# Where the hi parts of the gate weights are made, stream values in the gate's bank, and four buffers for FoX values

## The reference

```python
h = _rms(x, p['norm_mix'])
(fq, fk, fv, fg, bq, bk, bv, iq, ik, iw, cqa, ckva, ckpe) = jnp.split(h @ p['w_in'], ...)
...                                    # A: FoX, 6 heads, decay by a cumulated log gate
...                                    # B: DSA, 4 heads, indexer scores, top-k keys
...                                    # C: MLA, 6 heads, latent of 128, rotary key
ya = _over_query_blocks(fox_block, fq, qpos_b, cum[:, P:])
yb = _over_query_blocks(dsa_block, bq, qpos_b, iq, iw)
yc = _over_query_blocks(mla_block, q_nope, q_pe, qpos_b)
g = jax.nn.sigmoid((h @ p['w_gate']).astype(f32)).astype(x.dtype)
ga, gb, gc = jnp.split(g, 3, axis=-1)
x = x + (ga * ya @ w_fox_out + gb * yb @ w_dsa_out + gc * yc @ w_mla_out) @ p['w_o']
x = x + (jax.nn.silu(gt) * up) @ p['w_ffn_out']
```

## Time and profile before

| | |
|---|---|
| median of three runs | 2154.47 us |
| the profiled execution | 2154.84 us, its span 2153.0 us |
| PE busy | 2099.4 us, 98% |
| DVE busy | 1392.0 us, 65% |
| ACT busy | 968.7 us, 45% |
| PE on the chain that ended last | 89% of the span |
| chain: DVE 4%, ACT 3%, issue 2%, DMA 1% | |
| DMA | mean 97 GB/s |

### The profile page before, as it was taken

The page is one execution under the profiler, slowest core; times in us unless marked ns, Lnnn a source line. Parts: engine busy times, 40 slices in busy tenths (PEclk is TensorE's granted clock), DMA queues, the critical chain, the costliest instruction groups (busy, mean ns, idle before and its releaser), DMA issues.

```text
span 2153.0 us, 36860 instructions
## 1 busy us (share of the span) xinstructions
PE 2099.4 (98%) x13616; PEld 1883.8 (87%) x13616; DVE 1392.0 (65%) x2833; ACT 968.7 (45%) x2056; POOL 395.1 (18%) x287
## 2 busy tenths in 40 slices
PE   9999999999999999999999999999999999999999
PEld 8998768878979989989899887787889899899897
DVE  4567875545839838838445678766367497396493
ACT  4236766556425424314232467665663353243241
POOL 1120020200004314314011200203000142242230
PEclk9999999999999999999999999999999999999999
DMA  6233224132332222222232332241423222222222
GB/s 217 78 106 127 83 83 124 59 112 104 119 106 79 79 79 80 88 79 89 77 137 76 110 114 88 79 133 55 149 76 135 72 92 86 79 79 88 72 96 79
DMA packets 90681, 207.83 MB, mean 97 GB/s; under 512 B 20676, under 2 KB 46920, under 8 KB 90184
## 3 DMA queue, kind: packets, MB, share of 16 engines
q1 hardware_dynamic: 90504, 205.48, 28.3%
HBM read 181.50 MB, written 23.95 MB: 95 GB/s over the span
## 4 chain that ended last, share of the span: by engine, by line
PE 89%; DVE 4%; ACT 3%; issue 2%; DVEq 1%; POOL 1%; DMA 1%; SPq 0%; ACTq 0%
PE ps L879 28%; PE ps L925 16%; PE ps L1404 8%; PE ps L1406 8%; PE ps L1405 8%; PE ps L937 6%; PE ps L1096 2%; PE ps L1116 2%; PE ps L995 1%; PE ps L1014 1%; PE ps L1040 1%; PE ps L1210 1%; PE ps L1384 1%; PE ps L1175 1%; POOL rsq L1939 1%
## 5 line engine op out<-in xcount | busy, mean ns | idle before, releaser
L1465 ACT ACTIVATE w_hi<-raw 128x1024 fp32r<-128x1024 f32 (+4 forms) x172 | 171.0, 997 | 398.4 <-PE ps L879 369.4
L1994 DVE TENSOR_TENSOR w_lo<-raw,w_hi 128x1024 fp32r<-128x1024 f32 (+4 forms) x124 | 139.1, 1123 | 187.7 <-ACT w_hi L1465 183.8
L925 PE MATMUL ps<-h_hi,w_hi 128*128 128x320 f32 x768 | 246.8, 321 | 1.5 <-ACT g L1465 1.5
L925 PE MATMUL ps<-h_hi,w_lo 128*128 128x320 f32 x768 | 237.7, 310 | 0.0
L925 PE MATMUL ps<-h_lo,w_hi 128*128 128x320 f32 x768 | 237.6, 309 | 0.0
L1404 PE MATMUL ps<-th_hi,op_hi 128*128 128x320 f32 x640 | 198.1, 310 | 3.8 <-issue 3.8
L1939 POOL TENSOR_TENSOR rsq<-ssq,mhalf 128x12 f32<-128x12 f32 (+3 forms) x56 | 118.0, 2107 | 447.7 <-DVE ssq L2072 385.1
L1406 PE MATMUL ps<-th_hi,op_lo 128*128 128x320 f32 x640 | 198.2, 310 | 0.0
L1405 PE MATMUL ps<-th_lo,op_hi 128*128 128x320 f32 x640 | 198.0, 309 | 0.0
L879 PE MATMUL ps<-w_hi,act_hi 128*128 128x512 f32 x440 | 174.5, 397 | 0.0
L879 PE MATMUL ps<-w_lo,act_hi 128*128 128x512 f32 x440 | 174.4, 396 | 0.0
(11 more groups left out here) (376 smaller groups left out, 5327.5 us busy)
## 6 DMA issues: line engine op xcount, KB each, us to landing
raw<-in_weights SPq DMA_DIRECT2D x212, 512.0 KB, 3.3
gates<-gst SPq DMA_DIRECT2D x72, 160.0 KB, 1.8
g<-gates SPq DMA_DIRECT2D x12, 960.0 KB, 7.0
raw<-in_weights SPq DMA_DIRECT2D x24, 384.0 KB, 3.0
ktb<-in_cache_fox_kt SPq DMA_DIRECT2D x16, 384.0 KB, 4.8
vc<-in_cache_fox_v SPq DMA_DIRECT2D x16, 384.0 KB, 4.1
x_sb<-in_x_prompt SPq DMA_DIRECT2D x8, 512.0 KB, 4.6
out_y_prompt<-x_sb SPq DMA_DIRECT2D x8, 512.0 KB, 3.4
```

The lines of the kernel that those rows point to most:

```text
L925: mm = pe.matmul(ps[:, 5, 0:HALF], w[:, kk * P:(kk + 1) * P], h_pair[x][:, kk, half * HALF:(half + 1) * HALF], start=kk == 0 and n == 0, s ...
L1465: return act.activation(dst, src, ACT.Copy, scale=scale)
L1994: dve.tensor_tensor(low[:, 0:width], raw[raw_slot(c)][:, 0:width], high[:, 0:width].bitcast(F32), ALU.subtract).then_inc(lo_made.sem, 1)
```

## The change

Six edits:

1. Four of the jobs ahead of the attention (the transposes of DSA tile 2, and the two sums of the log gate) get banks 3 and 4, which nobody uses then (`EARLY`). The first indexer scores, which use banks 0 to 3, wait for them.
2. A stream's values may go to bank 5, the gate's, where the step has no gate half and the values before are in bank 4 (`OUT_BANK`). PE waits for the gate's last move, and the next gate half waits for the stream's output. By these rules it is items 57, 60, 80 and 82 of each layer. The others then wait for the last item in their own bank (`OUT_FREE`).
3. A fourth buffer for FoX values: stream 5 goes to the place of `wqb`, 6 to that of `bias`, 7 to `vc[1]`.
4. ACT makes `w_hi` of the next chunk at the end of its step, behind the exponential (`gate_next`), and no longer right behind `gate_move`. DVE's order is kept.
5. DVE makes both parts of `at_dsa`, first for the prompt columns and, after the last job, for the streams' columns; ACT's copy goes.
6. The buffers' semaphores are counted anew.

```diff
+EARLY = {JOB[_p] + _k: 3 + _k for _p in (("dsa", 2), ("gate_sums", 0)) for _k in range(2)}
...
-    BANK.append(5 if _j in THIRD else 6 + (_j - sum(_k < _j for _k in THIRD)) % 2)
+    BANK.append(5 if _j in THIRD else EARLY[_j] if _j in EARLY else 6 + (_j - sum(_k < _j for _k in THIRD)) % 2)
...
+OUT_BANK = [4] * N_ITEMS
+for _n in (*range(I_MLAS + 1, I_DSA), *range(I_DSAS, N_ITEMS - 1)):
+    if OUT_BANK[_n - 1] == 4 and not GATES_IN[_n + 3] and _n + 3 < N_ITEMS:
+        OUT_BANK[_n] = 5
+OUT_FREE = [max([0] + [VALUED[_m] + 1 for _m in range(_n) if VALUED[_m] != VALUED[_n] and OUT_BANK[_m] == OUT_BANK[_n]]) for _n in range(N_ITEMS)]
...
+                    if step == I_FOXS + 5:
+                        sp.wait_ge(tp_done.sem, tp_done.at(L, JOB["mla_expand", TT - 1] + 3))
+                        own_wait(sp, sp_tick)
+                        sp.dma_start(vc[2][:, :, :], past("fox_v", 5)).then_inc(vc_in[2].sem, 16)
                     if step == I_FOXS + 7:
...
-                        sp.dma_start(vc[2][:, :, :], past("fox_v", DECB - 1)).then_inc(vc_in[2].sem, 16)
+                        sp.dma_start(vc[3][:, :, :], past("fox_v", 6)).then_inc(vc_in[3].sem, 16)
+                    if step == I_FOXS + 8:
+                        sp.wait_ge(it_pv.sem, it_pv.at(L, I_FOXS + 4))
+                        own_wait(sp, sp_tick)
+                        sp.dma_start(vc[1][:, :, :], past("fox_v", 7)).then_inc(vc_in[1].sem, 16)
...
+                    if streams_out:
+                        pe.wait_ge(it_out.sem, it_out.at(L, streams_out[-1] + 1))
+                        streams_out.clear()
                     gates_begun[0] = k + 1
...
-                    pe.wait_ge(it_out.sem, it_out.at(L, i))
+                    bank = OUT_BANK[i]
+                    pe.wait_ge(it_out.sem, it_out.at(L, OUT_FREE[i]))
+                    if bank == 5:
+                        pe.wait_ge(g_moved.sem, g_moved.at(L, gates_begun[0]))
+                        streams_out.append(i)
...
+                        pe.wait_ge(tp_out.sem, tp_out.at(L, JOB["gate_sums", 0] + 2))
...
-                    if half:
-                        if k != GATE_LAST:
-                            hi(C_GATE + 2 + m, m % 2)
+
+                def gate_next(k):
+
+                    if k % 2 and k != GATE_LAST:
+                        hi(C_GATE + 2 + k // 2, k // 2 % 2)
...
                         exp(step)
-                act.wait_ge(tp_out.sem, tp_out.at(L, JOBS))
-                copy(h_hi[:, 6:8, :], at_dsa[:, :, :]).then_inc(at_hi.sem, 1)
+                    if step:
+                        for k in GATES_IN[step - 1]:
+                            gate_next(k)
                 hi(C_OUTS + 1, 1)
...
-                dve.wait_ge(at_hi.sem, at_hi.at(L, 1))
-                at_rest(6, 2, at_dsa)
+                dve.wait_ge(w_used.sem, w_used.at(L, C_OUTS))
+                dve.wait_ge(it_out.sem, it_out.at(L, I_DSAS))
+                for cols in (slice(0, SEQ), slice(SEQ, NTOK)):
+                    if cols.start:
+                        dve.wait_ge(tp_out.sem, tp_out.at(L, JOBS))
+                    dve.tensor_copy(h_hi[:, 6:8, cols], at_dsa[:, :, cols])
+                    dve.drain()
+                    last = dve.tensor_tensor(h_lo[:, 6:8, cols], at_dsa[:, :, cols], h_hi[:, 6:8, cols].bitcast(F32), ALU.subtract)
+                last.then_inc(at_lo.sem, 1)
```

More of the change, by code:

```diff
@@ L391, in build_program @@
         gate_new = home("gate_new", [102, P], BF16)
-        vc = [home(f"vc{k}", [P, 2, FH * HD], F32, "vc", 3072 * k) for k in range(2)] + [home("vc2", [P, 2, FH * HD], F32, "bias")]
+        vc = [home(f"vc{k}", [P, 2, FH * HD], F32, "vc", 3072 * k) for k in range(2)] + [home("vc2", [P, 2, FH * HD], F32, "wqb"), home("vc3", [P, 2, FH * HD], F32, "bias")]
         kpe = home("kpe", [P, TT, ROPE])
@@ L483, in build_program @@
         g_in, g_ready, acc_made, mix_half = sig("g_in", 16 * GATE_KEPT), sig("g_ready", KD), sig("acc_made", KD), sig("mix_half", KD)
-        at_hi, at_lo, vd_made = sig("at_hi", 1), sig("at_lo", 3), sig("vd_made", 1)
+        at_lo, vd_made = sig("at_lo", 3), sig("vd_made", 1)
         rows_free = sig("rows_free", 2)
@@ L496, in build_program @@
         lfr_made, grow_made = sig("lfr_made", 1), sig("grow_made", 1)
-        vc_in = [sig(f"vc_in{k}", 16 * (DECB // 2 - k)) for k in range(2)] + [sig("vc_in2", 16)]
+        vc_in = [sig(f"vc_in{k}", 16 * n) for k, n in enumerate((3, 3, 1, 1))]
         ktb_in, ctb_in = ([sig(f"{n}{k}", 16 * DECB // 4) for k in range(4)] for n in ("ktb_in", "ctb_in"))
@@ L725, in _ @@
                         own_wait(sp, sp_tick)
-                        sp.dma_start(vc[2][:, :, :], past("fox_v", DECB - 1)).then_inc(vc_in[2].sem, 16)
+                        sp.dma_start(vc[3][:, :, :], past("fox_v", 6)).then_inc(vc_in[3].sem, 16)
[3 more added lines that the diff above has]
+                        sp.dma_start(vc[1][:, :, :], past("fox_v", 7)).then_inc(vc_in[1].sem, 16)
                     b = step - (I_FOXS + 2)
-                    if 2 <= b < DECB - 1:
+                    if 2 <= b < 5:
                         sp.wait_ge(it_pv.sem, it_pv.at(L, I_FOXS + b - 1))
@@ L908, in _ @@
                 h_pair, mix_pair, act_pair = (h_hi, h_lo), (mix_hi, mix_lo), (act_hi, act_lo)
-                gates_begun, beside_gates = [0], []
+                gates_begun, beside_gates, streams_out = [0], [], []
                 def gate_half(k, first=0, end=KD):
@@ L1127, in values @@
                     if kind == "foxs":
-                        s = 2 if t == DECB - 1 else s
-                        pe.wait_ge(vc_in[s].sem, vc_in[s].at(L, 16 * (t // 2 + 1) if s < 2 else 16))
+                        s = (0, 1, 0, 1, 0, 2, 3, 1)[t]
+                        pe.wait_ge(vc_in[s].sem, vc_in[s].at(L, 16 * (1, 1, 2, 2, 3, 1, 1, 3)[t]))
                     if i == I_MLAS:
@@ L1145, in values @@
                             c = ckvc[:, t, j, :] if j < 2 else ckv_new[:, :]
-                            mm = pe.matmul(ps[0:96, 4, 0:KVL], pt[:, j * P:j * P + 96], c, start=first, stop=last)
+                            mm = pe.matmul(ps[0:96, bank, 0:KVL], pt[:, j * P:j * P + 96], c, start=first, stop=last)
                         if kind == "dsas":
                             v = dv_past[:, t, j, :] if j < 2 else v_dsa[:, TT - 1, :]
-                            mm = pe.matmul(ps[0:rows, 4, 0:HD], pt[:, j * P:j * P + rows], v, start=first, stop=last)
+                            mm = pe.matmul(ps[0:rows, bank, 0:HD], pt[:, j * P:j * P + rows], v, start=first, stop=last)
                     mm.then_inc(it_pv.sem, 1)
@@ L1615, in outputs @@
                         if kind == "dsas":
-                            last = copy(av[0:rows, t % 2, :].rearrange("p (r d) -> p r d", r=2), rows_bcast(ps[0:rows, 4, 0:HD], 2), over)
+                            last = copy(av[0:rows, t % 2, :].rearrange("p (r d) -> p r d", r=2), rows_bcast(ps[0:rows, OUT_BANK[i], 0:HD], 2), over)
                         else:
-                            last = copy(av[0:rows, t % 2, :], ps[0:rows, 4, 0:P], over)
+                            last = copy(av[0:rows, t % 2, :], ps[0:rows, OUT_BANK[i], 0:P], over)
                     last.then_inc(it_out.sem, pair_done(i))
@@ L1738, in _ @@
                 gate_move(1)
+                gate_next(1)
                 index_relus(0)
@@ L1744, in _ @@
                 gate_move(3)
+                gate_next(3)
                 fox_moves(2)
@@ L1749, in _ @@
                 gate_move(5)
+                gate_next(5)
                 for step in range(N_ITEMS + 6):
```

## The result

| | before | after |
|---|---|---|
| median of five runs | 2154.47 us | 2162.66 us (2160.71 to 2164.12) |
| span of the profiled execution | 2153.0 us | 2161.4 us |
| PE busy | 2099.4 us | 2103.1 us |
| span less PE busy | 53.6 us | 58.3 us |

The ratio is 1.0036, 95% interval 1.0023 to 1.0048: slower, by 8.2 us; 2159.3 was forecast, in a range up to 2167. The last line of the table is worth the most: PE's idle time grew by 4.7, where the sum of waits said 4.8.

What follows compares the result with a forecast made beforehand. PE, busy 98% of the span, was taken as the bound, so only its waits could change. Ten per-layer terms, gains and losses, summed to +2.4, +4.8 for two layers, giving 2159.3 us; range 2153 to 2164, outside ones 2147 to 2167.

Steps and rivals of the forecast that it cites:

- The clock: PE's granted clock, 0.50 for 3.4 us at 321.4: -3.4 or +3.4 possible, left out of the sum, put in the range.
- MLA prompt: MLA prompt steps: `probs_t` no longer stands behind `w_hi` on ACT, so PE's waits at L1096 shrink; -2.0 per layer.
- FoX prompt: FoX prompt steps: DVE's `w_lo` waits for the later `w_hi`, so `probs_t` comes late at two or three steps; +2.0 per layer.
- `sq_a`: Last FoX prompt step, before the latent's expansion: ACT's chain gets the full `w_hi` later, nothing covers it; +1.1 per layer.
- DSA prompt: Three DSA prompt steps: late `w_hi` and `w_lo` delay the gate half's move, and the next half waits; +2.7 per layer.
- FoX streams: FoX streams: fourth buffer removes the DMA wait, -1.7, but `av` comes about 2.2 later and values wait; +0.5 per layer.
- DSA streams: DSA streams: gate half 46 waits for item 80's late `av`, starting at 514.5 instead of 512.85; +1.6 per layer.
- MLA streams: MLA streams: items 57 and 60 go to bank 5, `w_hi` later at step 60; between -0.3 and +1.0, taken as +0.3.
- 1: Rival: the delay is hidden everywhere and only gains stay; -9.3 per layer, 2132.5 with two clock falls gone; chance 0.05.
- 2: Rival: gate halves cover the delay in FoX, latent and stream steps; only DSA's +4.3 stays; 2145.3; chance 0.12.
- 3: Rival: VectorE becomes the bound of the FoX prompt, five steps costing 6.0 instead of 3.1 per layer; 2165; chance 0.15.
- 4: Rival: SP's store keeps the DMA wait of 1.7, swallowing the 2.2 to 0.5; within 1 us, counted with the forecast.

Runs made afterwards that it cites:

- edit 4 alone: The kernel before with only ACT's `w_hi` moved behind the exponential: 2166.44 us, ratio 1.0056.
- the fifth experiment: The changed kernel with `w_hi` behind the exponential in the 24 MLA prompt steps alone, elsewhere right behind the gate half's move: 2139.88 us, ratio 0.9931.
- the late `w_lo`: The changed kernel, but DVE makes `w_lo` in the next step, behind that step's reciprocal and maxima; ACT's order kept: 2134.37 us, ratio 0.9907.

## Why the prediction was right, and where not

The direction and the mechanism held, and the time came near (2159.3 against 2162.7). That it came so near is in part luck. The clock, priced at nothing, cost 6.8, and the rest, priced at +4.8, came to +1.7 (the 8.5 of the matmuls lined up, less 6.8): two errors that worked against each other. The sign holds without the clock too, but +1.7 alone would hardly stand out of the noise. The mechanism is shown, not argued: undoing edit 4 gives 2143.0, edit 4 alone 2166.4, and taking DVE's reciprocal and maxima out from behind `w_lo`, with ACT's order untouched, 2134.4. Point by point:

- Early banks, -2.0 per layer: measured -2.6. Under-sized, since the waits were priced at their own length and the busy time behind them left out.
- MLA prompt, -2.0: measured -1.9, and -1.9 when tried alone. Right, with the reason: both waits of 1.05 stayed as 0.50, since `probs_t` then waits for the turns.
- L1162, -1.0: right (2.5 to 0.5 in both layers).
- FoX prompt, +2.0: new waits of 0.87 and 0.77 for `probs_t` in the first layer (0.92 and 0.77 in the second), 1.6 to 1.7. Right in place. The text said that L1096 would fall by about 4 in all; it fell by 0.4, since these waits are counted at the same line. That sentence contradicted my own sum.
- `sq_a`, +1.1: the wait grew by 1.6, from 0.79 to 2.39, but PE came 1.2 earlier; items 20 to 28 lose 0.3 to 0.4 only. Over-sized: a longer wait at a late gate is not lost time where PE arrives early.
- DSA prompt, +2.7: 2.3 to 2.4. The wait at the second place was 1.82, not 1.1, at the first 0.64, not 0.8; the third had none of its own at L943.
- FoX streams, +0.5: in the second layer, where the clock fell before and after, +0.9; in the first, where its fall at 321 went, -0.5. The step with the trade of waits was right.
- DSA streams, +1.6: the wait was 2.03 as forecast within 0.1 of PE's start, but with the fall behind it the stretch lost 3.0 to 3.1; without the 1.4 to 1.5 of that fall it is the 1.6 of the forecast.
- MLA streams, +0.3: lost 1.8 to 2.1, the furthest from its term. A wait of 1.61 at L1168 replaced two of 0.36 and 0.94 in the first layer (0.36 and 0.63 in the second), and behind it the clock fell in both layers, at 1.5 each. Without the falls the stretch lost 0.3 to 0.6. Edit 4 alone, with one bank and no fall there, lost 0.3 and 0.6 too; with the second bank but without edit 4 (a wait of 1.51, no fall) nothing was lost in either layer.
- Output split, -0.8: right; the wait at L937 is gone, and 0.3 of busy time behind it. (The 256 stream columns are a fifth of the 1280, not a quarter.)
- **The step that was mis-sized is the clock**, set at nothing because losses and gains seemed to balance. They did not: falls rose from three to eight and cost 6.8 us. That is twice the +3.4 that the prediction gave as the worst for it; the range held the result only because the rest was 3.1 lower than its sum. "PE's busy time is unchanged but for the clock" was wrong too, by the 3.2 of matmuls elsewhere.
- One reason was wrong: that edit 2 "turns a delay which PE could have worked through into a wait". Undoing it moved nothing (2162.69); PE stops at the values in its place. It is the late `av` that costs.
- The bound of 1.05 for DVE's waits did not hold as idle time (up to 3.5), since DVE also stands idle there for want of other work.

Of the rivals, 1 (2132.5) needed the delay hidden. It isn't, but the time is nearly that of the kernel in which it is (2134.4). 2 is out: the FoX prompt, the latent and the streams did show new waits. 3 (DVE the bound of the FoX prompt) is out: that stretch got 1.6 to 1.7 of new waits, not 6.0. 4 is out: the DMA wait did go.

What stays open: why the clock fell behind some waits and not behind others of the same length, and so how many falls an edit will bring; no run settles it. Part of a fall's price can be made up in waits behind it, as perhaps near 276 us, where the wait for `qa` shrank from 1.15 to 0.36 after the fall at 265; that was not tested. Executions of the one kernel also lie 3.4 us apart.

## What to carry to other kernels

When an instruction is moved back on one engine, look at the consumer that waits for it on another engine and list what is queued behind that consumer: a move that is free for the mover can stall an in-order queue, and the price shows at a third engine. The fix may be to move the consumer too: here moving `w_hi` alone cost 19.6 us, moving `w_lo` alone gained nothing, and both together gained 8.7. On an engine that is 98% busy, look behind each long wait for the granted clock: behind many of those of 1.5 to 2.4 us it fell, and that came on top of their length. And when two edits cost more together than apart, split the difference into idle and busy time first: here the idle time added up (10.9 and 11.7 us), and only the busy time did not.

## What the runs showed of the hardware that I had not expected

The same wait of 1.5 us before the same work was followed by granted clock 1.00 in one execution and 0.50 for 3.4 us in another (the rows of the fifth experiment); the fall cost 1.5 us. After the waits of 2.03, 1.61, 2.39 and 1.61 whose windows are shown above it was 0.50 to 0.53, the lower of the two levels of 1.2 and 2.4 GHz that the Trainium skill names ("TensorE: Matmul & The Clock Gate", section "What's actually happening"); the windows agree, with no third level in a whole stretch. After a second wait of 2.39 and after two of 1.82 in the same execution it stayed at 1.00, and the fall at 1392 stands behind waits of 0.77, 0.82 and 1.04 within 6 us, none of them long. With the late `w_lo`, whose attention stages have no wait above 1.41, the clock kept 1.00 there (PE busy 2091.9), and it kept it in the feed-forward too, behind a wait of 2.2 at L1427. So two kernels with the same waits, and two executions of one kernel (2137.79 and 2142.85 us at mean granted clocks of 1.000 and 0.997), can differ by a few us, and the reading is: take the granted clock of each stretch before a difference below 0.2% is given to an edit.
